# Memory keys and values of both layers moved into the block of the layer-0 norms

## The reference, cut to what matters

```python
def mem_kv(mem, norm_w, w_k, w_v):                      # mem (1, 256, 1024); w_k, w_v (1024, 1024)
    mn = rmsnorm(mem, norm_w)
    return (mn @ w_k).reshape(b, m, 4, 256), (mn @ w_v).reshape(b, m, 4, 256)
# layer 0, between the input projection u = h @ w_in and the attention:
ya = silu(layernorm(causal_dwconv(concat(conv_hist, glu)), ln_w, ln_b))
q = rmsnorm(c_q, q_norm_w) @ w_uq
ckv, krope = rmsnorm(kv[..., :128], kv_norm_w), rope(kv[..., 128:], pos)
# per layer i:
mk, mv = mem_kv(mem_prompt, norm_mem[i], x_w_k[i], x_w_v[i])     # both are also outputs
x = x + rmsnorm(cross_attn(rmsnorm(x, norm_pre_x[i]), mk, mv, ...), norm_post_x[i])
```

## Time and profile before

| | |
|---|---|
| median of the runs | 3494.05 us |
| profiled execution, own time | 3501.52 us |
| its span in the trace | 3499.9 us |
| mean granted TensorE clock | 0.899 of 2.4 GHz |
| busy share of the span: TensorE, VectorE, ScalarE, GpSimd | 82%, 44%, 22%, 16% |
| DMA, mean | 77 GB/s |

### The profile page before, as it was taken

One profiled execution on the slowest core, in us unless ns is written; L12 is line 12 of the kernel. 1 busy time (PEld: TensorE's weight loads), 2 busy tenths in 40 slices (PEclk: granted clock), 3 DMA queues, 4 the chain that ended last, 5 costly groups with the idle time before them and its releaser, 6 DMA issues. The chain is left out here.

```text
span 3499.9 us, 42303 instructions
## 1 busy us (share of the span) xinstructions
PE 2871.0 (82%) x16607; PEld 2245.1 (64%) x16607; DVE 1533.4 (44%) x2720; ACT 781.8 (22%) x1470; POOL 547.3 (16%) x436
## 2 busy tenths in 40 slices
PE   5993466668988789988799978966799996799889
PEld 5992334336767569956699956744555552499657
DVE  4996334444553310045356651035777773100353
ACT  3210123332222112222233222111222121122221
POOL 2220000003312112102122100000221221022011
PEclk8995688989998899999899989988799997899999
DMA  2110210006430221213022222136433310411151
GB/s 81 49 37 17 70 25 1 0 16 228 172 120 1 84 67 49 84 75 118 11 86 95 82 78 72 68 107 227 126 86 91 108 14 24 132 43 43 55 196 46
DMA packets 243204, 269.75 MB, mean 77 GB/s; under 512 B 44342, under 2 KB 198774, under 8 KB 237827
## 3 DMA queue, kind: packets, MB, share of 16 engines
q1 hardware_dynamic: 223234, 179.17, 17.1%
q0 software_dynamic: 16384, 75.77, 6.1%
q10 hardware_dynamic: 3456, 12.98, 0.9%
HBM read 227.03 MB, written 41.28 MB: 77 GB/s over the span
## 5 line engine op out<-in xcount | busy, mean ns | idle before, releaser
L305 PE MATMUL pp<-HH,WS_part 128*128 128x352 f32 x1776 | 573.1, 323 | 0.0
L303 PE MATMUL pp<-HH,WH 128*128 128x352 f32 x1344 | 436.0, 324 | 40.9 <-POOL WS_part L442 40.9
L304 PE MATMUL pp<-HT_part,WH 128*128 128x352 f32 x1344 | 434.1, 323 | 0.0
L305 PEld LDWEIGHTS pp<-HH,WS_part 128*128 128x128 f32 x1776 | 335.9, 189 | 0.0
L303 PEld LDWEIGHTS pp<-HH,WH 128*128 128x128 f32 x1344 | 254.0, 189 | 42.9 <-POOL WS_part L442 42.9
L2521 PE MATMUL OP<-oWO,YT 128*128 128x512 f32 (+1 forms) x576 | 255.5, 603 | 3.3 <-DVE XE L2648 3.3
L304 PEld LDWEIGHTS pp<-HT_part,WH 128*128 128x128 f32 x1344 | 254.1, 189 | 0.0
L442 POOL TENSOR_TENSOR WS_part<-WS,WH 128x1024 fp32r<-128x1024 f32 x56 | 141.9, 2534 | 651.0 <-ACT WH L393 651.0
L2521 PEld LDWEIGHTS OP<-oWO,YT 128*128 128x128 f32 (+1 forms) x576 | 104.8, 183 | 146.2 <-issue 142.5
L1843 DVE TENSOR_REDUCE xmx<-xS 128x4 f32<-128x1024 f32 x16 | 19.5, 1220 | 376.3 <-PE xS L1804 376.3
L773 DVE SCALAR_TENSOR_TENSOR CV<-GXP,cw,CV x240 | 172.8, 760 | 0.0
(11 more groups left out here) (476 smaller groups left out, 5538.0 us busy)
## 6 DMA issues: line engine op xcount, KB each, us to landing
WS<-x_w_qg SPq DMA_DIRECT2D x32, 512.0 KB, 4.0
HT<-cache_mem_k SPq DMA_DIRECT2D x16, 1024.0 KB, 8.0
HT<-cache_mem_v POOLq DMA_DIRECT2D x16, 1024.0 KB, 8.3
CBt<-cum_scratch SPq DMA_DIRECT2D x8, 2048.0 KB, 10.3
xbc_scratch<-oACC ACTq DMA_DIRECT2D x24, 528.0 KB, 2.7
WS<-o_w_in SPq DMA_DIRECT2D x24, 512.0 KB, 3.9
XT<-xbc_scratch SPq DMA_DIRECT2D x8, 1536.0 KB, 7.8
WS<-e_w_in SPq DMA_DIRECT2D x18, 512.0 KB, 4.0
```

The lines of the kernel that those rows point to most:

```text
L303: nc.tensor.matmul(out, wh, xh, start=start, stop=False)
L304: nc.tensor.matmul(out, wh, xl, start=False, stop=False)
L305: return nc.tensor.matmul(out, wl, xh, start=False, stop=stop)
```

## The change

`memory_keys_values`, `conv_states`, `qkv_norm` and `layer_norm_gate` are gone. One new block, `front`, does the work of the last three and the memory keys and values of both layers. Keys and values go to the outputs and to two scratch tensors in DRAM; `cross_attention` loads them back on SyncE, after the loads of its first eight weight blocks, and SyncE waits there for the landing. The memory's product is now a split product: for each of 16 half blocks (4 slices of the contraction x 512 columns, 1 MB of weights) SyncE loads into one of four slots in X, ScalarE rounds (`high`), VectorE (even half blocks) or GpSimd (odd ones) subtracts (`low`), and TensorE does 4 x 2 x 3 matmuls of 512 columns.

`in_project` has two more weight blocks: the latent keys (128 columns) and a block whose first 32 columns are the rotary keys. They are normed in the transposed layout, by sums with a matrix of ones, and turned for the outputs afterwards. Beside the projection SyncE loads the memory and the first three half blocks of weights (after the first eight weight blocks), and, after the last projection block, ScalarE and GpSimd norm the memory's rows.

The order of TensorE's list in `front`: transposes of the memory and of the convolution's states, sums for the layer norm, sums of squares of the queries, memory(0), sums for the keys, memory(1), memory(2), the rotary keys turned, memory(3), key_turn(0), memory(4), KR turned, memory(5), key_turn(1), CKT turned, memory(6), memory(7), variance sums, memory(8) to memory(15), with key_turn(4) after 11 and key_turn(5) after 13. VectorE's: states, T0, low(0), memory_low(0), centring (12), mean squares, reciprocal, QN (2), mean squares, low(2), reciprocal, four steps of a corrected inverse root, CKT, raw, low(4), rotary step, keys_out(0), low(6), KRT, keys_out(1), low(8), CKV, memory_low(1), variance, low(10), reciprocal, CV (4), low(12), keys_out(4), SG (4), low(14), keys_out(5). ScalarE's has the 16 `high`, the squares, three roots, the copies of the results out of PSUM (`pieces`) and the silu between them.

```diff
+                if n0 == start and "sync_first" in extra:
+                    extra["sync_first"](sp)
...
+        project(c, [(glu_col, 2, 4, glu, None), (gate_col, 2, 4, gates, None), (query_col, 1, 2, queries, None),
+                    (kv_col, 1, 2, keys, None)],
+                HT, HH, 2, {"vector": convolve, "sync_first": memory_loads, "scalar": memory_squares, "gpsimd": memory_rstd},
...
+                for b in range(8):
+                    for h in range(2):
+                        hb = 2 * b + h
+                        if hb + 4 < NHB:
+                            sp.wait_ge(fr_pe, hb + 1)
+                            sp.dma_start(W[hb % 4], mem_weights(hb + 4)).then_inc(fr_w[hb % 4], 16)
+                    l, cols = b // 4, slice((b % 2) * 512, (b % 2 + 1) * 512)
+                    for m in range(2):
+                        sp.wait_ge(fr_ev, 2 * b + m + 1)
...
+                        sp.dma_start(out, ring[:, piece, :]).then_inc(fr_out[piece], 16)
+                        if not is_key(b):
+                            sp.dma_start(vm_d[l][:, m, cols], ring[:, piece, :]).then_inc(fr_out[piece], 16)
+                    if b >= 1 and is_key(b - 1):
+                        keys_stored(b - 1)
...
+                for hb in range(1, NHB, 2):
+                    pool.wait_ge(fr_hi, hb + 1)
+                    nc.gpsimd.tensor_tensor(WL[hb % 4][:], W[hb % 4], WH[hb % 3][:], ALU.subtract).then_inc(fr_lp, 1)
...
+                def memory(hb):
...
+                    if h == 0 and b >= 2:
+                        pe.wait_ge(fr_ev, 2 * (b - 1))
+                    if hb % 2:
+                        pe.wait_ge(fr_lp, hb // 2 + 1)
+                    else:
+                        pe.wait_ge(fr_ld, hb // 2 + 1)
+                    for k in range(4):
+                        kt = 4 * h + k
+                        for m in range(2):
+                            cols = slice(m * P, (m + 1) * P)
+                            i = split_mm(MB[2 * (b % 2) + m][:], (MH[:, kt, cols], ML[:, kt, cols]),
+                                         (WH[hb % 3][:, k, :], WL[hb % 4][:, k, :]), kt == 0, kt == KT - 1)
+                    i.then_inc(fr_pe, 1)
...
+                def low(hb):
+                    dve.wait_ge(fr_hi, hb + 1)
+                    nc.vector.tensor_tensor(WL[hb % 4][:], W[hb % 4], WH[hb % 3][:], ALU.subtract).then_inc(fr_ld, 1)
...
+                def high(hb):
+                    act.wait_ge(fr_w[hb % 4], 16 * (hb // 4 + 1))
+                    if hb >= 3:
+                        act.wait_ge(fr_pe, hb - 2)
+                    nc.scalar.activation(WH[hb % 3][:], W[hb % 4], ACT.Copy).then_inc(fr_hi, 1)
...
-            memory_keys_values(l, KM, VM)
+
+            def back(sp):
+                sp.dma_start(KM[:], km_d[l]).then_inc(v_in, 16)
+                sp.dma_start(VM[:], vm_d[l]).then_inc(v_in, 16)
+                sp.wait_ge(v_in, 32 * (l + 1))
...
-                project(c2, [job(QT, 0, ACT.Copy), job(SGX, D, ACT.Silu)], HT, HH, 2)
+                project(c2, [job(QT, 0, ACT.Copy), job(SGX, D, ACT.Silu)], HT, HH, 2, {"sync_first": back})
```

More of the change, by code:

```diff
@@ L784, in build @@
[L784 to L790, removed]
-        with ExitStack() as c:
[L792 to L801, removed]
-            block = c.enter_context(nc.Block())
+    km_d = nc.dram_tensor("memk_scratch", (2, P, KT, MEM), F32).ap()
@@ L834, in _ @@
[L834 to L867, removed]
@@ new lines, in key_turn, with sums @@
+                def key_turn(b):
+                    n = 2 * (b // 4) + b % 2
+                    for m in range(2):
+                        pe.wait_ge(fr_ev, 2 * b + m + 1)
+                        if 2 * n + m:
+                            pe.wait_ge(fr_ke, 2 * n + m)
+                        for q in range(4):
+                            t = nc.tensor.transpose(TB[:, q * P:(q + 1) * P], ring[:, (2 * b + m) % 4, q * P:(q + 1) * P], ident[:])
+                        t.then_inc(fr_kt, 1)
+                def sums(banks, srcs):
+                    for g, (a, b) in enumerate(GROUPS):
+                        for n, src in enumerate(srcs):
+                            m = nc.tensor.matmul(banks[g][:, 0:GRP], ones[:], src[:, a:b], start=n == 0, stop=n == len(srcs) - 1)
+                        m.then_inc(k_sum, 1)
@@ L968, in _ @@
+                t.then_inc(s_stp, 1)
                 for g, (a, b) in enumerate(GROUPS):
+                    if g == 2:
+                        pe.wait_ge(s_sev, 1)
                     for ct in range(4):
-                        m = nc.tensor.matmul(ps[g][:, 0:GRP], ones[:], CV[:, ct, a:b], start=ct == 0, stop=ct == 3)
+                        m = nc.tensor.matmul(SB[g][:, 0:GRP], ones[:], CV[:, ct, a:b], start=ct == 0, stop=ct == 3)
                     m.then_inc(l_sum, 1)
-                pe.wait_ge(l_sq, 4)
@@ L973, in _ @@
-                for g, (a, b) in enumerate(GROUPS):
-                    for ct in range(4):
-                        m = nc.tensor.matmul(pv[g][:, 0:GRP], ones[:], sq[:, ct, a:b], start=ct == 0, stop=ct == 3)
-                    m.then_inc(l_var, 1)
+                pe.wait_ge(k_sq, 2)
+                pe.wait_ge(fr_te, 4)
+                sums([MB[2], MB[3], TB], [SQ[2], SQ[3]])
+                pe.wait_ge(fr_ml, 1)
+                memory(0)
+                pe.wait_ge(k_sq, 3)
+                pe.wait_ge(k_ms, 3)
@@ new lines, in _ @@
+                sums([MB[2], MB[3], TB], [SQ[4]])
+                memory(1)
+                pe.wait_ge(k_ms, 6)
+                memory(2)
+                for i, T in enumerate(TILES):
+                    t = nc.tensor.transpose(TB[0:T, i * ROPE:(i + 1) * ROPE], KRp[:, i * P:i * P + T] if i < NQ else KRs[:], ident[0:ROPE, 0:ROPE])
+                t.then_inc(k_rt, 1)
+                memory(3)
+                pe.wait_ge(k_raw, 2)
+                key_turn(0)
+                memory(4)
+                pe.wait_ge(l_cen, 12)
@@ new lines, in _ @@
+                memory(6)
+                memory(7)
+                pe.wait_ge(k_cev, 3)
+                for ct in range(4):
+                    pe.wait_ge(l_sq, ct + 1)
+                    for g, (a, b) in enumerate(GROUPS):
+                        m = nc.tensor.matmul(SB[g][:, 0:GRP], ones[:], SQ[ct % 2][:, a:b], start=ct == 0, stop=ct == 3)
+                    m.then_inc(l_var, 1)
+                pe.wait_ge(fr_ml, 2)
+                for hb in range(8, NHB):
+                    memory(hb)
+                    if hb in (11, 13):
+                        key_turn(4 if hb == 11 else 5)
@@ L978, in _, with memory_low @@
             @block.vector
             def _(dve):
+                def low(hb):
+                    dve.wait_ge(fr_hi, hb + 1)
+                    nc.vector.tensor_tensor(WL[hb % 4][:], W[hb % 4], WH[hb % 3][:], ALU.subtract).then_inc(fr_ld, 1)
+                def memory_low(l):
+                    for k in range(KT):
+                        dve.wait_ge(fr_mh, KT * l + k + 1)
+                        ins = nc.vector.scalar_tensor_tensor(out=ML[:, k, :], in0=T0[:, k, :], scalar=gm[:, l, k:k + 1],
+                                                             in1=MH[:, k, :], op0=ALU.mult, op1=ALU.subtract)
+                    ins.then_inc(fr_ml, 1)
@@ L980, in _ @@
+                dve.wait_ge(s_stp, 1)
+                nc.vector.tensor_copy(st[0:HIST, 0, :], TB[0:HIST, :])
+                nc.vector.tensor_copy(st[0:SMP, 1, :], SB[2][0:SMP, :]).then_inc(s_sev, 1)
+                low(0)
+                memory_low(0)
                 for g, (a, b) in enumerate(GROUPS):
@@ new lines, in _ @@
+                mean_square([MB[2], MB[3], TB], Rq, QL, 0)
+                dve.wait_ge(k_sd, 1)
+                dve_own.step(dve, nc.vector.reciprocal(Rq[:], Rq[:]))
+                for k in range(2):
+                    ins = nc.vector.scalar_tensor_tensor(out=QN[:, k, :], in0=QN[:, k, :], scalar=qg[:, k:k + 1],
+                                                         in1=Rq[:], op0=ALU.mult, op1=ALU.mult)
+                dve_own.step(dve, ins)
+                mean_square([MB[2], MB[3], TB], Rl, KV, 3)
@@ new lines, in _ @@
+                low(2)
+                dve.wait_ge(k_sd, 2)
+                dve_own.step(dve, nc.vector.reciprocal(Rq[:], Rq[:]))
+                for _ in range(2):
+                    dve_own.step(dve, nc.vector.tensor_tensor(Rl[:], Rl[:], Rq[:], ALU.mult))
+                dve_own.step(dve, nc.vector.tensor_scalar(Rl[:], Rl[:], -0.5, 1.5, ALU.mult, ALU.add))
+                dve_own.step(dve, nc.vector.tensor_tensor(Rq[:], Rq[:], Rl[:], ALU.mult))
+                nc.vector.scalar_tensor_tensor(out=CKT, in0=ckv, scalar=kg[:], in1=Rq[:], op0=ALU.mult, op1=ALU.mult).then_inc(k_ck, 1)
@@ new lines, in _ @@
+                dve.wait_ge(k_rt, 1)
+                dve.wait_ge(k_raw, 1)
+                nc.vector.tensor_copy(raw[:, 0:NQ], TB[:, 0:NQ * ROPE].rearrange("p (n a b) -> p n a b", n=NQ, a=2))
```

(34 more changed lines are left out.)

431 lines of the change are left out of this document (227 added, 204 removed).

## The result

The changed kernel takes 3362.24 us, the median of four runs (3357.24 to 3364.35), beside 3497.4 us for the kernel before, also the median of four. The ratio is 0.9605 with a 95% interval of 0.9575 to 0.9635. The forecast was 3360 us. The profiled execution took 3363.42 us, with a span of 3361.8 us against 3499.9 and a mean granted clock of 0.917 against 0.899.

A forecast was written before the change was run, and what follows sets the result against it. Replaced stretches were taken as chains of engines waiting for each other, memory blocks as exposed. Sum: -171.9 + 5.4 + (150 - 118.7) + 1 = -134.2 us, from 3494.05 to 3360 us, range 3333 to 3395.

The forecast's parts named there:

- What goes: Both memory blocks of cross attention leave the path: -85.9 and -86.0, together -171.9 us.
- The input projection: Its end, set by the convolution, comes later: two more subtractions 4.4 us, three small GpSimd instructions 1 us; +5.4 us.
- The late ninth weight block: Input projection: 4 MB queued ahead make it land some 9 us after issue instead of 4; TensorE may stand 1 to 3.5.
- F: Length of the new block in place of the three blocks of 118.7 us; taken as 150 us.
- VectorE's part: New block until the first keys are turned: VectorE's list of 53 us plus one GpSimd collision of 4.7, 57.7 us.
- TensorE's part and hand-overs: New block from memory(4) on, TensorE sets the pace for 84 us; some 20 hand-overs between engines add 2.3.
- Reading back: SyncE's wait for 2 MB in cross attention's projections stands about 10 us but costs 0 per layer (bounds 0 and 6).
- The clock term: Cross attention's projections start after a norm, so more runs at the lower clock: +1 us for both (bounds -2 and 4).
- 1: VectorE is the bound throughout the new block, blocked 38 us by GpSimd's subtractions: F = 165, 3375 us; chance 0.2.
- 2: Waits keep TensorE at its lower clock in the new block: F = 229, 3439 us; chance 0.07.
- 3: Weight loads stop running ahead, every half block waits for its own: F = 350, 3560 us, slower than before; chance 0.04.
- 4: Engine lists interlock better than counted in the new block, TensorE always fed: F = 126, 3336 us; chance 0.15.

The follow-up runs named there:

- e1: Kernel after with only VectorE's order changed: low(2), keys' mean square, rotary copies and first key copy earlier, second root in its own tile; 3352.35 us, ratio 0.9579.
- e4: Kernel after with the memory's products high times high alone, 128 matmuls instead of 384; 3341.4 us in one run.
- e3: Kernel after with all sixteen subtractions of the memory weights on VectorE, none on GpSimd; 3361.97 us, ratio 0.9603.
- e5: Kernel after with weight loads running two half blocks ahead instead of four; 3405.43 us in one run.
- e2: e1 with the first key copy ahead of the rotary step on VectorE; 3353.08 us, ratio 0.9589.
- e10: e2 with the second key turned after memory(6), its copy after low(8), and all sixteen subtractions on VectorE; 3358.42 us, ratio 0.9603.

## Why the prediction was right

- **What goes**: 85.9 and 86.0 us, both gone in full.
- **The input projection**, +5.4 forecast: +3.3 (+3.2 to +4.5 over all runs with the full convolution). The last matmul ends at 285, the memory's norm at 292.5 instead of 296. The late ninth weight block never showed: it landed 6.4 us behind its issue, for 9 counted, and TensorE was busy for all of 100 to 180, so the 1 to 3.5 us of standing were wrong and without effect.
- **F**, 150 forecast: 147.8. VectorE's part, 57.7 to the first key copy: 55.9 (304.97 to 360.84). It held two GpSimd collisions, of 1.7 and 4.3 us, where I had counted one of 4.7. Without them the list took 49.9 us, for 53 counted: two errors that partly cancel. The waits were 5.5 us before memory(2) for 6, and 3.3 and 4.3 at the key turns for 9. TensorE's part and hand-overs, 84 + 2.3: 86.2. Tail, 6: 5.7. e1's 10.6 us show VectorE's list as the cause of the first part, and the 21 us of e4 show TensorE's products as the cause of the second. The second part wasn't at full clock from its start, as the prediction has it, but behind 369.
- **Engine sums**: TensorE 117.5 forecast, 125.3 measured at a mean clock of 0.93; ScalarE 61, 62.1; GpSimd 38, 38.6; VectorE 87, 96.3, the difference being GpSimd's holds.
- **Reading back**: 0 forecast, 0 measured; SyncE stood the 10 us named. The clock term of +1 was -0.4 with it.
- **Rivals**: 1 falls as a bound, by e3, though e4 shows it as the next one. 2 falls by the clock, 0.93 over the block. 3 falls by the four slots and has its price from e5. 4 (F = 126, TensorE always fed) didn't come: TensorE waited 13.1 us in its three long waits. A better order goes half of that way: 137.1.

The -134.2 us stand beside -135.2 of the medians. The closeness of this last figure is partly luck. The stretches that the change touches sum to -139.9 us in the traces, 5.7 more than forecast: 2.1 of them from the input projection, 2.2 from F and 1.4 from the clock term. The profiled execution of the kernel before was used with an offset to the median of 7.5 us, which with a fourth run is 4.1, and unrelated stretches move by 7 us between executions.

## What to carry to other kernels

Work that depends on nothing belongs where a chain leaves the engine that it needs idle; what it costs there is read by running the chain without it (75.9 us against 147.8). The order of the lists was worth 10.6 us in one place and nothing in the three further steps tried: each moved the wait on. So after a step that pays, look for the engine whose list all waits name, here VectorE. An offloaded elementwise operation is not free: where it meets a two-input operation of VectorE, one of the two stands until the other has ended. Yet taking all eight back to VectorE (e3) won nothing.

## What the hardware showed that was not expected

The size of VectorE's operation doesn't matter to a hold: 0.31 us became 4.57 (e1), 1.26 became 5.54 (after) and 1.32 became 5.75 (e2); each stood until the GpSimd subtraction that it met, of 4.6 us, had ended, and then ran. Where VectorE comes late in the subtraction the hold is its rest: 1.7 us at the query scaling (after). GpSimd waits as well: its subtraction that started during one of VectorE's took 6.25 us (e1). Operations from PSUM and the reciprocals weren't held (0.93 and 6.75 us beside one, after). The Trainium skill ("SBUF — State Buffer", section SBUF: two separate sides) describes an exclusive lock on a port pair for the whole instruction. These numbers agree with it, and a price in shares of bandwidth would have been wrong.

A short wait can cost TensorE more than itself. Behind the wait of 5.5 us in the kernel after, eight matmuls started 0.43 us or more apart instead of 0.23, at a granted clock of 0.51 (338.4 to 342.4). With the waits of 3.3 and 4.3 us it fell again, and rose behind them:

```profile
356.00:362.00 6.00, 1.69 (x9) 1.31 (x8) 4.70 (x9) 0.00 (x0) 0.00 (x0) 0.50 0.47 169
362.00:369.00 7.00, 7.00 (x24) 5.50 (x23) 2.89 (x2) 0.00 (x0) 0.00 (x0) 0.70 0.19 77
369.00:378.00 9.00, 8.06 (x43) 6.41 (x42) 2.08 (x4) 3.52 (x4) 4.62 (x1) 1.00 0.46 123
```

The Trainium skill ("TensorE: Matmul & The Clock Gate", section HAM oscillation) tells of bursts of matmuls that start at the lower rate after a wait for a load; here the waits were for VectorE. The length of a wait alone doesn't say whether the clock falls: a wait of 2.12 us in e3 was followed by eight matmuls 0.43 us apart, one of 2.12 us in e10 by none.
